# Output projection: sums of the fourth operand and a gain load moved ahead of the late products

## The reference

```python
hn   = _rmsnorm(h, pre_norm_gain)
proj = einsum('bsd,de->bse', hn, w_in)              # q, k, v, g_a, u_b, g_b: 1024 features each
y_a  = stick_breaking(heads(q), heads(k), heads(v)) * silu(g_a)   # 8 heads x 128
y_b  = multiscale_pool(u_b, w_pool, pool_scale) * silu(g_b)       # windows 2, 4, 8, 16
mix  = concatenate([y_a, y_b])                      # 512 x 2048
out  = einsum('bse,ed->bsd', mix, w_out)            # 2048 x 2048
h    = h + _rmsnorm(out, post_norm_gain)            # mean of squares over all 2048 columns
```

## Time and profile before

| | us |
|---|---|
| median of three runs | 712.13 |
| lowest to highest | 711.82 to 712.38 |
| the profiled execution, its time | 711.82 |
| the same, its span from the first to the last instruction | 710.1 |
| PE busy | 700.5 (99%) |
| DVE busy | 601.4 (85%) |
| ACT busy | 448.4 (63%) |
| mean granted PE clock, share of full | 0.997 |

### The profile page before, as it was taken

One profiled execution on the slowest core, in us unless ns is written; L12 is line 12 of the kernel. 1 busy time (PEld: TensorE's weight loads), 2 busy tenths in 40 slices (PEclk: granted clock), 3 DMA queues, 4 the chain that ended last, 5 costly groups with the idle time before them and its releaser, 6 DMA issues. The chain is left out here.

```text
span 710.1 us, 10201 instructions
## 1 busy us (share of the span) xinstructions
PE 700.5 (99%) x3840; PEld 611.0 (86%) x3840; DVE 601.4 (85%) x775; ACT 448.4 (63%) x615; POOL 81.0 (11%) x98
## 2 busy tenths in 40 slices
PE   8999999999999999999999999999999999999995
PEld 6888888888888888888888888888888889988884
DVE  3499987998789898988898978899898998596787
ACT  4775576666676756676775677765687546543461
POOL 0000000110020110011120011030002001001001
PEclk9999999999999999999999999999999999999998
DMA  8965436557646666655755756657655519988985
GB/s 291 395 201 138 132 104 180 161 164 206 176 114 180 164 177 180 174 158 152 189 149 174 180 158 174 161 139 183 186 162 196 151 26 275 284 215 257 279 321 238
DMA packets 46898, 133.86 MB, mean 189 GB/s; under 512 B 4480, under 2 KB 14720, under 8 KB 45952
## 3 DMA queue, kind: packets, MB, share of 16 engines
q1 hardware_dynamic: 37680, 105.92, 43.7%
q0 software_dynamic: 9024, 27.27, 22.2%
q10 hardware_dynamic: 144, 0.01, 0.0%
HBM read 128.99 MB, written 4.19 MB: 188 GB/s over the span
## 5 line engine op out<-in xcount | busy, mean ns | idle before, releaser
L2052 PE MATMUL ps<-a_ops,w_hi 128*128 128x512 f32 x1120 | 270.8, 391 | 0.0
L2052 PEld LDWEIGHTS ps<-a_ops,w_hi 128*128 128x128 f32 x1120 | 205.5, 188 | 39.5
L1219 DVE TENSOR_TENSOR raw_lo<-raw,w_hi 128x1024 fp32r<-128x1024 f32 x155 | 188.8, 1225 | 17.6 <-ACT w_hi L722 17.3
L722 ACT ACTIVATE w_hi<-raw 128x1024 fp32r<-128x1024 f32 x155 | 163.2, 1055 | 63.8 <-PE ps L2052 35.6
L2060 PEld LDWEIGHTS ps<-a_ops,raw_lo 128*128 128x128 f32 x1120 | 145.7, 191 | 6.3
L2060 PE MATMUL ps<-a_ops,raw_lo 128*128 128x256 f32 x1120 | 149.9, 283 | 0.0
L1909 POOL DMA_DIRECT2D raw<-w_heads x40 | 35.0, 874 | 313.0 <-DMA raw<-w_heads 255.5
L1962 PE MATMUL ps<-w_hi,a_ops 128*128 128x256 f32 (+1 forms) x208 | 69.1, 332 | 0.0
L1964 PE MATMUL ps<-w_hi,a_ops 128*128 128x256 f32 (+1 forms) x208 | 69.1, 332 | 0.0
L1963 PE MATMUL ps<-raw_lo,a_ops 128*128 128x256 f32 (+1 forms) x164 | 54.5, 332 | 0.0
L1678 DVE TENSOR_TENSOR raw_lo<-raw,w_hi 128x1024 fp32r<-128x1024 f32 x28 | 34.1, 1223 | 18.0 <-ACT w_hi L1092 17.9
(11 more groups left out here) (242 smaller groups left out, 1054.9 us busy)
## 6 DMA issues: line engine op xcount, KB each, us to landing
raw<-w_heads SPq DMA_DIRECT2D x100, 512.0 KB, 4.2
raw<-w_heads POOLq DMA_DIRECT2D x40, 512.0 KB, 5.7
raw<-w_out SPq DMA_DIRECT2D x38, 512.0 KB, 6.1
raw<-w_v SPq DMA_DIRECT2D x15, 512.0 KB, 10.1
x_rows<-x SPq DMA_DIRECT2D x6, 1024.0 KB, 11.8
mix<-xT SPq DMA_DIRECT2D x16, 256.0 KB, 10.0
raw<-w_out POOLq DMA_DIRECT2D x8, 512.0 KB, 9.0
raw_more<-w_out SPq DMA_DIRECT2D x8, 512.0 KB, 6.5
```

The lines of the kernel that those rows point to most:

```text
L722: act.activation(hi_slot(g), raw_slot(raw, slot), ACT.Copy).then_inc(w_hi_done, 1)
L1219: dve.tensor_tensor(raw_slot(raw_lo, slot), raw_slot(raw, slot), hi_slot(g).bitcast(F32), ALU.subtract).then_inc(w_split, 1)
L2052: mm = pe.matmul(dst, hi[:, k * P:(k + 1) * P], a_ops[:, a:a + SEQ], start=k == 0 and p in (0, 1, 5), stop=stop and k == KH - 1, skip_grou ...
```

## The change

On DVE and ACT the fourth operand's sums (`s4_sums`, `s_hi_of(q, 3)`, `s_lo_of(q, 3)`), which stood in turn 0 of the loop over t, now stand ahead of it, pair by pair, with the split of steps 0 and 1 between the first pairs. The split of step 2, which was ahead of them, is after them. The four gain products `rows_gain(s, 0)` on DVE go from turns 4 to 7 to turn 0, the four squares on ACT from turns 1 and 2 to turn 0, and DVE waits for the gain rows just ahead of the loop. The four `s3` splits go from turns 3 and 4 (two each) to turns 0 to 3 (one each). `a_keep_of(0)` stays at turn 2, but behind `late_hi_of(4)` and no more ahead of it. On SP the load of the gain rows goes ahead of the loads of steps 7 and 8. In SBUF `o_sum` moves from the place of `raw_last` to that of the third slot of `w_hi` (which is why hi of step 2 now waits for `s_split` 12; SP's wait for the same ahead of step 9 stays), and `out_ms` gets a place of its own.

```diff
@@ SBUF
+        with ExitStack() as outs:
+            sb("w_hi_pad", [P, (HI_SLOTS - 1) * QUARTER], scope=outs)
+            o_sum = [sb(f"o_sum{i}", [P, SEQ], scope=outs) for i in range(2)]
         w_hi = sb("w_hi", [P, HI_SLOTS * QUARTER], F32R)
...
+        out_ms = sb("out_ms", [P, TT])
...
-        half, row_root, out_ms = ms_col[:, 0:1], ss_col[:, 0:1], rstd_col
+        half, row_root = ms_col[:, 0:1], ss_col[:, 0:1]
...
-        with ExitStack() as outs:
-            o_sum = [sb(f"o_sum{i}", [P, SEQ], scope=outs) for i in range(2)]
@@ SP
             sp.wait_ge(o_chunk_done, KK)
+            sp.dma_start(post_gain_rows[:, :],
+                         post_gain.partition_broadcast(P)).then_inc(rows_gain_loaded, 16)
             load_late(RAW_SLOTS)
             load_late(RAW_SLOTS + 1)
-            sp.dma_start(post_gain_rows[:, :],
-                         post_gain.partition_broadcast(P)).then_inc(rows_gain_loaded, 16)
             sp.wait_ge(s_split, 3 * PAIRS)
             load_late(RAW_SLOTS + 2)
@@ ACT, late_hi_of
                 if t < HI_SLOTS:
                     act.wait_ge(step_done, STEPS)
+                    if t == HI_SLOTS - 1:
+                        act.wait_ge(s_split, 3 * PAIRS)
@@ ACT, the loop
-            late_hi_of(0)
-            late_hi_of(1)
+            for q in range(PAIRS):
+                s_hi_of(q, 3)
+                if q < 2:
+                    late_hi_of(q)
             for t in range(LAST - 2):
-                if t == late_end("A", 0) + 1:
-                    a_keep_of(0)
                 late_hi_of(t + 2)
                 if t + 2 >= LAST - PAIRS:
                     late_hi_of(t + 2 + PAIRS)
                 if t == 0:
-                    for q in range(PAIRS):
-                        s_hi_of(q, 3)
-                if t in (1, 2):
-                    rows_square(2 * t - 2, 0)
-                    rows_square(2 * t - 1, 0)
-                if t in (3, 4):
-                    s3_hi_of(2 * t - 6)
-                    s3_hi_of(2 * t - 5)
+                    for s in range(TT):
+                        rows_square(s, 0)
+                if t == late_end("A", 0) + 1:
+                    a_keep_of(0)
+                if t < PAIRS:
+                    s3_hi_of(t)
@@ DVE, the loop
-            late_lo_of(0)
-            late_lo_of(1)
+            for q in range(PAIRS):
+                s4_sums(q)
+                s_lo_of(q, 3)
+                if q < 2:
+                    late_lo_of(q)
             dve.memset(half, 0.5).then_inc(half_set, 1)
+            dve.wait_ge(rows_gain_loaded, 16)
             for t in range(LAST - 2):
...
                 late_lo_of(t + 2)
                 if t == 0:
-                    s4_sums(0)
-                    for q in range(1, PAIRS):
-                        s4_sums(q)
-                        s_lo_of(q - 1, 3)
-                    s_lo_of(PAIRS - 1, 3)
-                if t in (3, 4):
-                    s3_lo_of(2 * t - 6)
-                    s3_lo_of(2 * t - 5)
-                if 4 <= t < 4 + TT:
-                    if t == 4:
-                        dve.wait_ge(s_summed, 5 * PAIRS)
-                        dve.wait_ge(rows_gain_loaded, 16)
-                    rows_gain(t - 4, 0)
+                    dve.wait_ge(s_summed, 5 * PAIRS)
+                    for s in range(TT):
+                        rows_gain(s, 0)
+                if t < PAIRS:
+                    s3_lo_of(t)
```

## The result

The changed kernel takes **721.20 us** in the median of four runs (720.00 to 721.95) beside 712.11 (711.82 to 712.38) for the kernel before. The ratio is 1.0125 with a 95% interval of 1.0112 to 1.0138: 9.1 us slower. The forecast was 716.8 us and its range ended at 720.0. The sign and the two waits came as forecast; half of the loss came from two places that had no share in the sum.

What follows compares the result with a forecast made beforehand. PE was taken to bound the kernel, with no wait to win in this stage. The profiled 711.82 us plus 4.7 of waits gave 716.5, stated as 716.8 us against the median of 712.13; range 715.2 to 720.0.

Steps and rivals of the forecast that it cites:

- The sign: Whole kernel: slower by over 0.2% at 0.95, within 0.2% at 0.04, faster at 0.01.
- the two waits: New PE waits ahead of steps 2 and 3, about 1.6 and 3.1 us, 4.7 together.
- the sum: PE's total loss at steps 2 and 3, equal to the gain rows' time from issue to landing, taken as 4.7 us.
- The end ... is not touched but for the address of `out_ms`: From the last matmul on, nothing was expected to differ; the new address got no price.
- The clock: Rival: PE falls to half clock around the wait ahead of step 3, costing 3 to 6 us on top; chance 0.07.
- those 3.4 us: At the kernel's end, PE's time without a matmul, 702.6 to 706, before half clock; cited against the clock's fall.
- The chain from the gain rows to step 3: From the gain rows' landing through DVE and ACT to PE's start of step 3: 8.4 us.
- Steps 8 and 9: Late steps expected to bring no further PE wait; a third wait there would show the forecast wrong.
- The floor of 3.4: Rival: turn 0's work alone makes PE wait 3.4 us, even with free gain rows; 715.5 us, chance 0.10.
- Part 2: Work in turn 0: PE waits 0.2 us at step 2, and product 0's copy comes 3.4 us late for step 3.

Runs made afterwards that it cites:

- e1_shift32: Kernel before, with only a separate place for out_ms, so everything allocated behind it lies 32 bytes higher; 715.66 us beside 712.19.
- e10_gains_back: Changed kernel with out_ms in its old place and DVE's gain products and their wait back at turns 4 to 7; 716.93 us beside 712.84.
- e11_squares_back: Changed kernel, out_ms in its old place, DVE's gain products and wait back at turns 4 to 7, ACT's squares at turns 1 and 2; 716.22 us beside 712.84.
- e5_sums_only: Kernel before with only the sums ahead of the loop, o_sum in w_hi's third slot and the gain load first; addresses from x_hi on unchanged; 713.01 us beside 712.24.
- e4_wait_at_gains: Changed kernel with out_ms in its old place and DVE's wait for the gain rows moved to just ahead of the first gain product; 716.48 us, ratio 1.0056.
- e8_all256: Kernel before with a_ops, mix, raw and w_hi 128 bytes higher, x_hi and all behind it where they were; 714.89 us beside 712.24.

## Why the prediction was wrong

**What failed is one sentence and one chance.** "The end ... is not touched but for the address of `out_ms`" looked only at who writes `out_ms`, and gave the new address no price. In fact the declaration moves all that lies behind it by 32 bytes, which costs 3.3 us ahead of step 0 and 3.5 alone in e1_shift32. It was in the diff, and the order says nothing of it. No row of before has another placement, so the price could not be read there. But it could be bounded: the forms of matmul in that trace, all of 128x512, have means from 389 to 398 ns (two forms that stand behind the waits at the start apart), and 6 or 7 ns on each of the 384 matmuls on x is 2.3 to 2.7 us. I did not ask why like matmuls differ.

**The clock** did fall, which had 0.07 and 3 to 6 us. The chance was too small and the price too high. Of 15 executions of the changed kernel eight have a mean clock of 0.994 or 0.995 and take 721.3 to 722.0; seven have 0.996 or 0.997 and take 720.0 to 720.7. The slow matmuls span 3.2 us, about a step, but one of 256 columns starts every 0.213 us there against 0.12: 1.4 us, which is also the distance of the two groups. "Both waits are shorter than those 3.4 us" was no protection: with waits of 1.52 and 2.83 us and one step of 2.87 between them it fell in eight of 15. A first wait of that length is not needed either. With 0.52 and 2.72 us (e10_gains_back) five of nine executions have a mean of 0.995 or less, with 0.52 and 2.27 (e11_squares_back) four of ten, with 0.5 alone (e5_sums_only) none of ten. Where the clock dips is seen only in the two profiles of such executions; for the others it is inferred from their mean clock and time. A low mean by itself is no proof: kernels without a new wait have it now and then too (three of 77 executions of the kernel before, at 716.0 to 716.5 us, some 4 us above its median), and for that no profile was kept.

**What held.** The load landed 4.7 us after its issue (4.5 to 5.0 in the variants), as taken. Two waits came, the first released by DVE's lo, the second by ACT's copy of product 0, 1.52 and 2.83 us against 1.6 and 3.1. The chain from the gain rows to step 3 was 602.07 - 593.83 = 8.2 (DVE starts 0.03 after the landing, at 593.86) against 8.4, and the sum 4.35 against 4.7. DVE stood idle 1.41 us, as said (589.2 to 590.6). Steps 8 and 9 brought no wait, nor did the end differ. The floor of 3.4 was measured at 3.34 (e4_wait_at_gains). At the old placement and full clock the changed kernel would thus be at about 718.35 - 1.4 = 717.0, against the 716.8 forecast.

**One reason was right in size and incomplete in cause.** Part 2 put the wait ahead of step 3 down to "four gain products". The runs show that the copy behind hi of step 4, the splits and the squares give 2.72 of the 2.82 without them. In the sum it made no difference, because both chains end at almost the same time.

**The account.** 9.1 us in the median: 3.3 to 3.5 placement, 4.35 the two waits, 1.4 the clock in those executions in which it falls (half of them). What is left in the profiled execution, 0.65 behind step 0, is partly placement too (0.4 in e1_shift32 over the same stretch, the only profile to compare); for the last 0.2 I have no row.

## What to carry to other kernels

When a change adds or removes a tensor in SBUF, even one of 16 bytes, list whose addresses move and look at the stages that read both from what moved and from what stayed; compare the mean duration of their matmuls by form before anything else. A transfer moved ahead is worth only what waits for it, and a wait put ahead of work that does not need it charges its whole landing time to that work. An engine's queue with an important copy at its end is read for everything ahead of the copy, not only for the largest item.

## What the runs showed of the hardware

- The rate of an fp32 matmul of 512 columns depends on where the tensors in SBUF lie relative to each other. On w and x, against the kernel before: 389 ns unchanged, 391 with `x_hi` and all behind it 64 bytes lower, 395 with them 128 lower, 396 with them 32 higher (starts 0.2267 against 0.2333 us apart), and 389 again with the other group 256 higher. The neighbouring matmul has part in it: the form on `q_hi` and `k_hi`, whose own distance never changed, took 396 ns (before), 388 (e1_shift32) and 392 (e8_all256).
- With two waits of PE of 1.5 and 2.8 us and one busy step of 2.9 us between them, eight of 15 executions have the low mean clock; the one profiled is at half clock for some 3 us, from 0.7 us after the second wait. A lone wait of 0.5 us did it in none of ten.
- One DMA of 1 MB that writes one row to 128 partitions lands after 4.5 to 5.0 us when it is issued first, and after 7.9 to 9.1 us behind two loads of 512 KB.
